# Gathering each expert's token rows over all 128 partitions, and putting them back in slot order by a matmul

## What is computed

```python
h2 = rmsnorm(x, norm2_g).reshape(bsz * L, D)
eidx, gates = hier_route(h2, r1_w, r1_b, r2_w, r2_b)    # top-1 group, then top-2 of its 8 experts
...
def expert_block(args):
    xb, e = args
    h = jax.nn.silu(xb @ w1[e]) * (xb @ w3[e])          # w1, w3: 1024 x 512
    return h @ w2[e]                                    # w2: 512 x 1024
...
x = x + segment_sum(out[dest] * g_sorted[:, None], tok, num_segments=T)
```

## Time and profile before

| | us |
|---|---|
| median of 3 runs | 1025.72 (1023.95 to 1026.57) |
| the profiled execution | 1025.62 |
| its span, first to last instruction | 1024.0 |
| PE busy | 921.0 (90%) |
| DMA queue q1 (SP), share of 16 engines' span | 60.6% |
| DMA queue q0 (POOL), same | 8.1% |

### The profile page before, as it was taken

How to read it: one execution, slowest core, us unless ns; L and a number is a source line. 1 busy time by engine, 2 the same in 40 slices (tenths; PEclk the granted TensorE clock), 3 DMA queues, 4 the chain that set the end, 5 groups by cost and what they waited for, 6 DMA issues and landing times. The chain is left out here.

```text
span 1024.0 us, 24939 instructions
## 1 busy us (share of the span) xinstructions
PE 921.0 (90%) x10522; PEld 587.5 (57%) x10522; DVE 247.6 (24%) x760; ACT 111.0 (11%) x172; POOL 157.4 (15%) x239
## 2 busy tenths in 40 slices
PE   5999999999999973999999999989988999898940
PEld 2545545455455542876777677657556685674620
DVE  1434452454534553410000000000000000000006
ACT  0211110111101110001010101010010010010004
POOL 1000000000000002112222222212112122112110
PEclk9999999999999995999999999999989999998985
DMA  8760010100101063999999999999999999999938
GB/s 340 277 251 21 22 41 0 41 21 21 41 0 43 39 247 98 394 366 390 363 387 363 370 367 369 368 372 376 368 390 375 379 384 380 355 389 363 326 70 322
DMA packets 57935, 258.22 MB, mean 252 GB/s; under 512 B 11410, under 2 KB 12490, under 8 KB 40853
## 3 DMA queue, kind: packets, MB, share of 16 engines
q1 hardware_dynamic: 47740, 238.54, 60.6%
q0 software_dynamic: 10144, 18.95, 8.1%
HBM read 234.55 MB, written 24.60 MB: 253 GB/s over the span
## 5 line engine op out<-in xcount | busy, mean ns | idle before, releaser
L1186 PEld LDWEIGHTS ps<-hT,big 128*64 128x64 f32 x8192 | 286.4, 138 | 40.1 <-issue 28.6
L1186 PE MATMUL ps<-hT,big 128*64 128x64 f32 (+8 forms) x8192 | 294.7, 233 | 14.7 <-DMA big<-in_exp_w 7.9
L1202 PE MATMUL ps<-big,poolT 128*64 128x512 f32 (+8 forms) x512 | 233.8, 609 | 11.3 <-DMA big<-in_exp_w 7.5
L1083 PE MATMUL ps<-big,hT 128*128 128x512 f32 x384 | 169.9, 602 | 3.3 <-DMA big<-in_w_in 1.9
L1202 PEld LDWEIGHTS ps<-big,poolT 128*64 128x64 f32 (+8 forms) x512 | 75.1, 152 | 145.8 <-issue 135.2
L985 DVE TENSOR_TENSOR poolT<-u,ps 128x256 f32<-128x256 f32 (+8 forms) x32 | 15.1, 472 | 505.1 <-PE ps L1186 467.4
L1083 PEld LDWEIGHTS ps<-big,hT 128*128 128x128 f32 x384 | 73.2, 193 | 94.6 <-issue 88.5
L545 POOL DMA_INDIRECT x_rows<-xn,sidx x32 | 49.4, 1545 | 385.3 <-ACT xn L695 363.3
L695 ACT ACTIVATE xn<-ps,gslot 64x1024 f32<-64x1024 f32 (+8 forms) x32 | 35.5, 1110 | 456.0 <-PE ps L1202 240.8
L525 POOL DMA_INDIRECT slot_table<-ids,dest x18 | 18.7, 1038 | 328.2 <-DVE dest L807 271.9
L1140 PE MATMUL ps<-big,yT 128*128 128x512 f32 x128 | 56.4, 593 | 0.9 <-DVE yT L874 0.9
(11 more groups left out here) (168 smaller groups left out, 469.1 us busy)
## 6 DMA issues: line engine op xcount, KB each, us to landing
big<-in_exp_w SPq DMA_DIRECT2D x192, 1024.0 KB, 25.9
big<-in_w_in SPq DMA_DIRECT2D x4, 1536.0 KB, 13.5
big<-in_w_out SPq DMA_DIRECT2D x2, 2048.0 KB, 14.9
x_rows<-xres SPq DMA_DIRECT2D x8, 512.0 KB
h_rows<-xn SPq DMA_DIRECT2D x8, 512.0 KB, 2.7
big<-x_rows SPq DMA_DIRECT2D x8, 512.0 KB, 7.3
out_y_prompt<-big SPq DMA_DIRECT2D x8, 512.0 KB, 2.9
xres<-in_x_prompt SPq DMA_DIRECT2D x1, 3072.0 KB, 11.1
```

The lines of the kernel that those rows point to most:

```text
L1083: last = pe.matmul(ps[0:m, bank, :], hT[:, k, 0:m], win[:, k, part * AW:(part + 1) * AW], start=(k == 0), stop=(k == KD - 1))
L1186: last = pe.matmul(out[c * w:(c + 1) * w, j, 0:m], up_weights(n)[:, k, j * P + c * w:j * P + (c + 1) * w], xT[:, 4 * half + k, 0:m], start ...
L1202: last = pe.matmul(ps[0:m, 5 + cols, :], hhT[:, 2 * half + k, 0:m], down_weights(n)[:, k, cols * 512:(cols + 1) * 512], start=(half + k == ...
```

## The change

The gather's indices come from a second copy of the table, `spread`, read by four DMAs, so that slot w*32 + i of an expert lies on partition 4*i + w. Every gather now has 128 index rows and fills `xg[s]` over all partitions; unused slots are skipped as before. `pick` is the identity with its columns in the matching order, so that a matmul of the rows with its first `m` columns gives the turned rows in slot order. DVE makes it once, during the second tile, in the space of `band_first`. PE calls `matmul` where it called `transpose`. `tabs` stays for the gates and the scatter.

```diff
+WAYS = 4
-SMALL = max(c[1] for _, _, c in CLASSES)
...
+        spread = sb("spread", [P, NE, 2], I32)
...
+        pick = band_first[:, 0, :]
...
             sp.wait_ge(table_stored, 16 * 2 * NT)
+            for w in range(WAYS):
+                sp.dma_start(spread[w:P:WAYS, :, :].rearrange("p e c -> p (e c)"),
+                             slot_table.rearrange("(r e) c -> r (e c)", e=NE)[w * P // WAYS:(w + 1) * P // WAYS, :])\
+                    .then_inc(spread_in, 16)
             sp.dma_start(tabs.rearrange("p e c -> p (e c)")[0:CAP, :],
                          slot_table.rearrange("(r e) c -> r (e c)", e=NE)[0:CAP, :]).then_inc(tabs_in, 16)
...
-            def fetch(b, s, e, m):
-
-                pool.tensor_copy(gidx[s][0:m, :], entries(e, m, 0)).then_inc(gidx_ready, 1)
+            def fetch(b, s, e):
+
+                token = spread[:, e, 0:1] if isinstance(e, int) else spread[:, bass.ds(e, 1), 0]
+                pool.tensor_copy(gidx[s][:, :], token).then_inc(gidx_ready, 1)
...
-                gather(xg[s][0:m, :], gidx[s][0:m, :], rows_in[s])
+                gather(xg[s][:, :], gidx[s][:, :], rows_in[s])
...
-                        fetch(b + 2, s, after[s], SMALL if s else m)
+                        fetch(b + 2, s, after[s])
...
+            pool.wait_ge(spread_in, 16 * WAYS)
+            for s in range(2):
+                fetch(s, s, FIRST + s)
             pool.wait_ge(tabs_in, 16)
-            for s in range(2):
-                fetch(s, s, FIRST + s, CAP)
...
                     dve.wait_ge(base_set, 1)
+                    dve.wait_ge(pooled, 1)
+                    dve.tensor_copy(pick.rearrange("p (w i) -> p w i", w=WAYS),
+                                    ident.rearrange("p (i w) -> p w i", w=WAYS)).then_inc(pick_made, 1)
...
+            def turn_rows(x, m, done):
+
+                xs = x[:, :].rearrange("t (p k) -> t k p", k=KD)
+                for c in range(KD):
+                    last = pe.matmul(ps[:, c // 4, (c % 4) * P:(c % 4) * P + m], xs[:, c, :], pick[:, 0:m],
+                                     start=True, stop=True, skip_group_check=True)
+                last.then_inc(done, 1)
...
-                        turn(xg[1 - s], max(caps_of[1 - s], SMALL), xgT_done)
+                        turn_rows(xg[1 - s], caps_of[1 - s], xgT_done)
...
-            turn(xg[0], CAP, xgT_done)
+            pe.wait_ge(pick_made, 1)
+            turn_rows(xg[0], CAP, xgT_done)
```

More of the change, by code:

```diff
@@ L262, in build @@
         tabs_in = sem("tabs_in")
+        spread_in = sem("spread_in")
+        pick_made = sem("pick_made")
         chunk_in = [sem(f"chunk_in{c}") for c in range(2 * CH)]
```

## The result

The kernel with the change takes **1119.12 us** (median of 4 runs, 1117.88 to 1122.53) against 1025.34 us before (4 runs, 1023.95 to 1026.57): ratio 1.092, interval 1.091 to 1.094. The forecast was 1029.5, the range 1020 to 1039. It is slower, as forecast, but by 94 us and not by 4. The profiled execution took 1120.08 us with a span of 1118.5, so 94.5 us of span are to be found.

A forecast was written before the change was run, and what follows sets the result against it. The prediction took the DMA engines, more closely the slowest of the 16, to bound the stage, with PE close. Sum: 1025.6 + 1.1 + 2.9 - 1 + 1 (a few more single waits) = 1029.6, say 1029.5 us; range 1020 to 1039.

The forecast's parts named there:

- What bounds the kernel: Stage from 403 to 986 us: bound by the DMA engines, 36.8 us per pair, with PE busy 34.5.
- The turn's price: PE's turn of eight matmuls: 1.80 us instead of 0.95, +0.85 a turn, 27.2 us of PE work over 32 turns.
- The cover: PE's 30.2 us of idle time and some 7 us of slow clock absorb the 27.2 us of turns: nothing added.
- The way back of the table: Stage start: POOL waits for four DMAs instead of one, delaying first gathers, first turn and weights: +1.1 us.
- What each engine gets: The 16 DMA engines: total unchanged, wide gathers add rows to the slowest engine, two pairs at 1.4 us: +2.9 us.
- even engines: Rival, chance 0.18: narrow gathers hold back the slowest engine; spread out, weights land earlier until PE bounds: 1016.7 us, -8.9.
- narrow scatters and gathers evened each other out: Pairs 13 and 14: both came in turn and could fall on different engines; wide gathers add to the scatter's engines.
- count of most loaded engines: Through all pairs by the skill's rule: within about 2 us up to pair 9, 1 to 8 us worse after pair 12.
- The waits near the end: Last pairs: a wide gather lands earlier and shortens PE's waits, at most 3.5 us to win, four turns against it: -1 us.
- PE or a dry queue: Rival, chance 0.12: turns cost over 0.85 us more or late `used` starve the engines: +12 and 1.1 us, 1039 us.
- The point that it named for its test: Dry-queue rival's sign: a weight load lands within 6 us of its issue between 430 and 500 us; 11.2 us before.
- the forecast's own signs of being wrong: Latencies short to the end, DMA share under 1, or PE's weight waits gone and the stage shorter than 583 us.

The follow-up runs named there:

- a_transpose: The changed kernel with the turn's eight matmuls run in transpose mode against all 128 columns of the permuted identity: 1018.52 us, 0.9945; on another chip 1017.28 us.
- a_contig: The changed kernel with 128 neighbouring channels as each turn matmul's stationary operand instead of every eighth one: 1035.48 us, ratio 1.010.
- b_rows128: The kernel before with 128-row gathers after the first two, no spread, no `pick`, turns unchanged: 1014.99 us, ratio 0.991.
- b_matmul128: b_matmul with 128 rows and 128 columns in every turn, gathers still narrow, on a second chip: 1079.09 us, ratio 1.053.
- t_first: a_transpose with `tabs` read first and serving the first two gathers, the four `spread` reads behind it: 1001.33 us, 0.979; repeated on another chip 1013.72 us.
- b_matmul: The kernel before with eight float32 matmuls against the identity in place of the turn's transposes, gathers still narrow: 1138.18 us, ratio 1.111.

## Why the prediction was wrong

*What bounds the kernel* held for the kernel before: engines first, PE close behind. a_transpose shows it, where wider gathers freed 6 to 8 us.

*The turn's price* is the step that failed, as a term mis-sized: "I take 1.80". It measured 3.86: 2.9 us more than before and not 0.85, 94 us and not 27 over 32 turns. The rows I costed it by had the same engine, type and size, but a stationary operand of neighbouring elements. "It is the second pass that costs" was right and not all: a_contig has the second pass at 1.84 us, and the step of eight elements doubles each loading. The upper bound of 1.85 was no bound, because the nearest row differed in the one property that decided. I had not weighed the Trainium skill's rule on lines of 16 bytes (SBUF — State Buffer, "Door 1: The DMA port swizzle"), which spoke against this choice.

*The cover.* I counted 30.2 us of idle time and 7 us of slow clock as cover. The idle time went as thought (22 of 30). The slow clock did not go with the waits, it grew by 19.5 us: I had taken it to follow only from waiting, and in the changed kernel it comes behind slow turns without any wait. The 7 us themselves were a guess that no row gave; the down-projections' sum puts them at 8. And the cover would not have held at the forecast's price either: the same 27 us of turns cost 17 us between a_transpose and a_contig.

*The way back of the table* was forecast at +1.1. Counted from SP's first issue it measured +1.2 for the first turn and +1.6 for the weights, near enough, but partly by luck: I took an issue of SP at the price of a weight load, and each of these reads costs 0.61 us.

*What each engine gets* had the wrong sign: +2.9 forecast. b_rows128, which changes only this, is 9.9 us faster (0.991, 0.988 to 0.994). The rival "even engines" had -8.9, near in number, but by a slow engine relieved, and that isn't shown. My argument that narrow scatters and gathers evened each other out doesn't hold, and nor does the count of most loaded engines by the Trainium skill's rule (DMA: Bandwidth & Descriptors, "Why a DMA increments its semaphore by 16 and not by 1") that would have given 1028 to 1035. I had held the total fixed, so that only the slowest engine's share could count. The window of b_rows128 from 480 to 950 us, against the earlier trace rows:

```profile
480.00:950.00 470.00, 453.04 (x7542) 320.00 (x7540) 32.10 (x52) 39.14 (x52) 109.08 (x156) 0.99 1.01 386
```

The engines are as busy as before (1.01 and 1.02) and move 386 GB/s instead of 374. A MB of weights took 39.8 engine-us in place of my 41.5 (87.7% of 16 engines over 470 us for 165.80 MB); on the second chip it was 43.6 with narrow gathers (b_matmul128) and 39.2 to 39.8 with wide ones. So the time for a byte fell, in all engines together, and the gain needs no slow engine. Why wide gathers make the bytes cheaper, and which engine was the slowest, is in no view and stays open.

*The waits near the end* (-1 us). In the changed kernel PE waited for no late gather. In b_rows128, with turns of 0.95 us again, it waited 7.4 us for two of them, so a wide gather doesn't land early enough by itself.

*The rivals.* "PE or a dry queue", at 0.12, had the mechanism and named its condition, a turn dearer than 0.85 us more. Its price of 12 us rested on the same 1.80 and fell with it. The point that it named for its test, a load landing within 6 us between 430 and 500 us, was not reached (8.6 to 10.6 us from 450 to 500); the forecast's own signs of being wrong were: latencies short to the end, a share of 0.91. My forecast fails by its own list, where turns of 1.8 us and a share of 1.02 stood.

## What to carry to other kernels

Before the form of a PE instruction is exchanged, price it by a row with the same access pattern, not only the same size: here a transpose of strided float32 data cost 0.12 us, an ordinary matmul with that stationary operand 2 x 0.24, eight times a block. If rows have to be permuted, a call marked as a transpose against a full permutation of 128 x 128 does it at the transpose's price. Where small gathers share the engines with large loads, give them 128 index rows, unused ones skipped: that alone, two edited places, is 1% here. The versions to keep are t_first, the fastest on both chips where it ran, or b_rows128, which was within 1.3 us of it on the one chip where both ran.

## What the runs showed of the hardware

- A float32 loading of the stationary operand for an ordinary matmul: 195 and 202 ns at steps of 1 and 2 elements, 325 and 336 ns at 4 and 8. A transpose at a step of 8: 195 ns.
- Behind turns of 3.9 us the granted clock fell to 1.2 GHz for about 3.4 us in the middle of uninterrupted work (0.95 over 470 us in the changed kernel, 0.91 in b_matmul). In b_matmul128, whose turns were as long over 128 rows and columns, it stayed at 1.00, on another chip.
- The same 256 matmuls of 64 columns took 7.68 us on one chip and 8.7 us on two others; those of 88 columns took 9.9 us on either. t_first took 1001.3 us on the first and 1013.7 us on one of the others, the kernel before 1024.3 to 1025.6 us on all three.
- A read of 32 rows onto every fourth partition costs SP 0.61 us of issue, one onto 96 neighbouring ones 0.35. The latter took 0.58 us when it stood behind the four others, so the step may not be all of it.
- With gathers of 128 index rows the DMA engines, busy as before, moved 386 to 389 GB/s where it had been 374.
